# A two-block transformer kernel: output norms, gate and first key and query tiles taken token tile by token tile

## The reference, cut to what matters

```python
h = h + rms_norm(y, norm_post[i])        # y = o @ w_out, 1024x1024
e = p[i] @ ple_w[i]                      # 256 features -> 1024
g = sigmoid(h @ ple_gate[i])             # 1024x1024
h = h + rms_norm(g * e, ple_norm[i])
```

## Time and profile before

| | us |
|---|---|
| median of 3 runs (1077.23 to 1079.66) | 1077.61 |
| the profiled execution | 1082.48 |
| its span on the core | 1080.7 |

### The profile page before, as it was taken

The page is one execution under the profiler, slowest core; times in us unless marked ns, Lnnn a source line. Parts: engine busy times, 40 slices in busy tenths (PEclk is TensorE's granted clock), DMA queues, the critical chain, the costliest instruction groups (busy, mean ns, idle before and its releaser), DMA issues.

```text
span 1080.7 us, 20360 instructions
## 1 busy us (share of the span) xinstructions
PE 1036.0 (96%) x8578; PEld 870.3 (81%) x8578; DVE 485.1 (45%) x668; ACT 558.8 (52%) x888; POOL 747.4 (69%) x470
## 2 busy tenths in 40 slices
PE   7999999999999999999999999999999999999796
PEld 6887898999989969999998456699977787777665
DVE  3125176431146876421145848544467344223433
ACT  6548365444446956444443434222335368578744
POOL 5986468998865678998883175440327777998863
PEclk9999899999999999999999999999999999999999
DMA  9771345556545644555556335300004463554241
GB/s 360 269 252 60 126 160 178 183 192 191 182 164 169 200 170 162 187 194 181 190 189 225 132 123 177 129 4 4 5 23 156 154 211 134 199 176 133 82 162 43
DMA packets 46218, 168.36 MB, mean 156 GB/s; under 512 B 5648, under 2 KB 5904, under 8 KB 45872
## 3 DMA queue, kind: packets, MB, share of 16 engines
q1 hardware_dynamic: 43616, 158.02, 43.2%
q0 software_dynamic: 2512, 9.05, 2.5%
HBM read 166.00 MB, written 1.05 MB: 155 GB/s over the span
## 4 chain that ended last, share of the span: by engine, by line
PE 82%; ACT 7%; DVE 6%; issue 2%; DMA 1%; SPq 0%; POOL 0%; DVEq 0%; ACTq 0%
PE psum L443 29%; PE psum L480 18%; PE psum L702 16%; PE psum L2255 5%; PE psum L455 3%; PE psum L2403 1%; PE psum L252 1%; ACT high_r L962 1%; DMA h<-x 1%; PE psum L1989 1%; PE psum L2143 1%; DVE arena L1516 1%; PE psum L227 1%; PE psum L2321 1%; ACT arena L1009 0%
## 5 line engine op out<-in xcount | busy, mean ns | idle before, releaser
L792 POOL TENSOR_TENSOR ring_r<-ring,high_r 128x512 fp32r<-128x512 f32 (+1 forms) x374 | 647.0, 1762 | 157.9 <-ACT high_r L962 144.1
L962 ACT CAST high_r<-ring 128x1024 fp32r<-128x1024 f32 x250 | 257.8, 1049 | 187.0 <-DMA ring<-w 182.9
L480 PE MATMUL psum<-x_high,high_r 128*128 128x256 f32 x640 | 183.0, 286 | 2.8 <-DVE x_low L316 2.8
L480 PE MATMUL psum<-x_low,high_r 128*128 128x256 f32 x640 | 181.7, 284 | 0.0
L480 PE MATMUL psum<-x_high,ring_r 128*128 128x256 f32 x640 | 181.7, 284 | 0.0
L674 DVE TENSOR_TENSOR arena<-arena 128x512 f32<-128x512 f32 x32 | 47.7, 1490 | 193.9 <-ACT arena L650 193.8
L480 PEld LDWEIGHTS psum<-x_high,high_r 128*128 128x128 f32 x640 | 123.5, 193 | 4.1 <-issue 3.5
L480 PEld LDWEIGHTS psum<-x_low,high_r 128*128 128x128 f32 x640 | 123.6, 193 | 0.5
L480 PEld LDWEIGHTS psum<-x_high,ring_r 128*128 128x128 f32 x640 | 123.5, 193 | 0.0
L443 PE MATMUL psum<-high_r,x_high 128*128 128x512 f32 x256 | 102.3, 399 | 7.2 <-POOL ring_r L787 2.4
L702 PE MATMUL psum<-high_r,zz_high 128*128 128x512 f32 x256 | 99.8, 390 | 1.3 <-DVE zz_low L681 1.3
(11 more groups left out here) (360 smaller groups left out, 1826.2 us busy)
## 6 DMA issues: line engine op xcount, KB each, us to landing
ring<-w SPq DMA_DIRECT2D x288, 512.0 KB, 3.3
row<-rows POOLq DMA_DIRECT2D x14, 512.0 KB, 6.3
arena<-relt SPq DMA_DIRECT2D x2, 1536.0 KB, 14.0
h<-x SPq DMA_DIRECT2D x1, 1024.0 KB, 11.3
arena<-lora POOLq DMA_DIRECT2D x2, 512.0 KB, 7.1
out<-h SPq DMA_DIRECT2D x2, 512.0 KB, 2.6
arena<-xT SPq DMA_DIRECT2D x1, 768.0 KB, 6.6
con<-consts SPq DMA_DIRECT2D x1, 529.0 KB, 7.0
```

What stands on the lines that cost most here:

```text
L480: ins = nc.tensor.matmul(out, a, b, start=(k == 0 and q == 0), stop=(k == KT - 1 and q == 2))
L792: ins = nc.gpsimd.tensor_tensor(low(m)[:, part], raw(m)[:, part], read(high(m))[:, part], ALU.subtract)
L962: nc.scalar.copy(high(m), raw(m)).then_inc(high_made, 1)
```

## The change

`out_by_token` walks the second output tile for all of t = 0 and then all of t = 1; sum, root, reciprocal and addition to `h` follow for each token tile by itself. The embedding product is split in two column halves, of which the first needs only the first output tile read; the three matmuls without use go. The transposes of `h` are made for one token tile at a time in banks of four blocks (`pe_token_transposes`), t = 0 between the halves, t = 1 inside the first gate tile, which is now walked by token tile too. The first key and query tiles are walked t = 0 of the keys, transposes of t = 1, t = 0 of the queries, t = 1 of the keys, t = 1 of the queries; `kv_high`, `q_high`, `kv_low` and `q_low` make the parts by token tile with 128x128 instructions. A piece of a tile that is walked by token tile is given back (`piece_used`) in the pass of t = 1. The matmuls without use are now 22 ahead of the transposes of t = 0 and 12 behind them. `posted` moves in the arena, and in `embed_dve` the gain of the second column half comes after the variance.

```diff
+            def out_by_token(first, e_n):
+                for t in range(NT):
+                    for i in range(4):
+                        piece_ready(pe, 4 * (first + 1) + i)
+                        ins = pe_piece_of_tile(pe, first + 1, i, 2, xT2, t)
+                        if t == 1:
+                            ins.then_inc(piece_used, 1)
+                    if t == 0:
+                        ins.then_inc(out_pass, 1)
...
             def embed_pe(tile, e_n, T):
-                hold_clock(4, 3)
-                pe.wait_ge(part_sq, 8 * e_n + 4)
-                pe.wait_ge(part_gain, 4 * e_n + 4)
...
+                embedding_half(tile, e_n, 0)
+                pe_token_transposes(pe, T, h, 0, posted_rows)
+                embedding_half(tile, e_n, 1).then_inc(piece_used, 4)
+                for t in range(NT):
+                    for i in range(4):
+                        if t == 0 and i == 3:
+                            pe_token_transposes(pe, T, h, 1, posted_rows)
...
-            hold_clock(0, 8)
-            pe_transposes_of_tile(pe, T_H7, h, 0, token_ready(0))
-            hold_clock(0, 14)
-            pe_transposes_of_tile(pe, T_H7, h, 1, token_ready(1))
+            hold_clock(0, 22)
+            pe.wait_ge(gate_act, 1)
+            pe_token_transposes(pe, T_H7, h, 0, embedded_rows)
+            hold_clock(0, 12)
...
+            for t in range(NT):
+                for c in range(2):
+                    for i in range(4):
+                        piece_ready(pe, 4 * (W_KVQG + c) + i)
...
+                        ins = pe_piece_of_tile(pe, W_KVQG + c, i, KVQG_BANK[c], KVQG_X[c], t)
+                        if t == 1:
+                            ins.then_inc(piece_used, 1)
+                    if (t, c) == (0, 0):
+                        pe.wait_ge(gate_act, 3)
+                        pe_token_transposes(pe, T_H7, h, 1, embedded_rows)
```

On ScalarE, `out_norm` has the casts of the first two gate pieces behind the root of each token tile, and the stretch behind the embedding reads:

```diff
+                    if e_n == 0 and t == 1:
+                        kv_high(0)
...
             out_norm(6, W_OUT_A, 0)
             embed(7, W_PLE0, 0, T_H6)
             split_until(4 * W_KVQG + 5)
+            q_high(0)
             split_until(4 * W_KVQG + 8)
+            kv_high(1)
+            q_high(1)
```

More of the change, by code:

```diff
@@ L1844, in out_gain @@
-            def out_gain(i, first, e_n, name):
-                g_ = row_of(name)
[L1847 to L1852, removed]
-                        nc.vector.tensor_tensor(posted[:, t, hl], psum[:, 2 * c + t, :], g_[:, hl], ALU.mult).then_inc(part_gain, 1)
-                dve.wait_ge(part_gain, 4 * e_n + 4)
-                add_normed(i, 2 * e_n)
@@ new lines, in kv_low @@
+            def kv_low(t):
+                tt = slice(t * P, (t + 1) * P)
+                for b in range(4):
+                    dve.wait_ge(xb_high_made, 4 * t + 2 * (b // 2) + 2)
+                    for k in (2 * b, 2 * b + 1):
+                        ins = nc.vector.scalar_tensor_tensor(out=XBL[:, k, tt], in0=token_filling(4 * T_H7 + 2 * t + b // 2)[:, k % 4, :],
+                                                             scalar=c8("kv_norm")[:, k:k + 1], in1=read(XBH[:, k, tt]),
+                                                             op0=ALU.mult, op1=ALU.subtract)
+                    ins.then_inc(xb_low_made, 1)
@@ new lines, in q_low @@
+            def q_low(t):
+                tt = slice(t * P, (t + 1) * P)
+                for q in range(2):
+                    g = 4 * T_H7 + 2 * t + q
+                    dve.wait_ge(tp_act, ACT_BANKS[g + 1])
+                    for k in range(4 * q, 4 * q + 4):
+                        ins = nc.vector.scalar_tensor_tensor(out=XL[:, k, tt], in0=token_filling(g)[:, k % 4, :],
+                                                             scalar=c8("norm_pre1")[:, k:k + 1], in1=read(XH[:, k, tt]),
+                                                             op0=ALU.mult, op1=ALU.subtract)
+                    ins.then_inc(tp_dve, 1)
@@ L2388, in _, with embedding_half @@
             gate_piece(1, 3)
+            def out_by_token(first, e_n):
[5 more added lines that the diff above has]
+                            ins.then_inc(piece_used, 1)
+                    if t == 0:
+                        ins.then_inc(out_pass, 1)
+            def embedding_half(tile, e_n, c):
+                pe.wait_ge(part_sq, 8 * e_n + 2 * c + 2)
+                pe.wait_ge(part_gain, 4 * e_n + 2 * c + 2)
+                for k in range(2):
+                    for t in range(NT):
+                        ins = nc.tensor.matmul(psum[:, 2 * c + t, :], pT_sb[:, k, t * P:(t + 1) * P],
+                                               raw(4 * tile + k)[:, c * HALF:(c + 1) * HALF], start=(k == 0), stop=(k == 1))
+                return ins
@@ L2411, in embed_pe @@
+                embedding_half(tile, e_n, 1).then_inc(piece_used, 4)
+                for t in range(NT):
+                    for i in range(4):
+                        if t == 0 and i == 3:
+                            pe_token_transposes(pe, T, h, 1, posted_rows)
+                        piece_ready(pe, 4 * (tile + 1) + i)
+                        bank_out(pe, 4 * T + 2 * t + i // 2)
                         ins = pe_piece_of_tile(pe, tile + 1, i, 4, xT2, t)
-                    ins.then_inc(piece_used, 1)
+                        if t == 1:
+                            ins.then_inc(piece_used, 1)
```

201 lines of the change are left out of this document (112 added, 89 removed).

## The result

| us | before | changed |
|---|---|---|
| median | 1077.88 (1077.23 to 1079.66, 4 runs) | 1088.46 (1085.46 to 1093.11, 4 runs) |
| profiled execution | 1082.48 | 1087.55 |
| its span | 1080.7 | 1085.5 |
| mean granted clock | 0.994 | 0.992 |

A forecast was written before the change was run, and what follows sets the result against it. TensorE, in matmuls for 96% of the span, was taken as the bound, so time is won only where it stands still or works for nothing. 7.8 lost less 2.1 won gives +5.7 us, 1077.61 to 1083.3, range 1078.0 to 1086.0.

The forecast's parts named there:

- Output tile and embedding, first boundary: Second output tile to gate's end, first boundary: tile ends 0.4 late, gate ends at 885.4, 1.7 us won.
- From the gate to the keys: Gate's end to first key matmul: matmuls without use decide, keys start at 894.2 against 896.62, 2.4 us won.
- The supply of pieces: First key and query passes: POOL supplies 243 to 247 late, TensorE stands about one us before each of four or five passes.
- The release of the ring, and POOL behind it: From the keys' second pass: late release of 240 and 241 delays evacuation, rotation and piece 252; 7.8 us lost.
- Load 3.3: Ring release step: load assumed to take 3.3 us before cast 1.05 and evacuation 0.7, giving 919.1.
- Second boundary: Output tile to gate at the second boundary: no 0.4 wait for POOL, 2.1 us won.
- A (faster): Rival: POOL has the low part of 247 by 904.6, both boundary wins stand, 1074.0 us; chance 0.08.
- B (no change): Rival: supply in time, only late release counts, or slack behind 939 returns most of the 7.8; 1078.0 us; chance 0.14.
- C (the clock falls): Rival: clock falls in the starved stretch from 899 to 910, delaying release of 241 by 1.7; 1085.0 us; chance 0.14.
- The sum: Whole kernel: +7.8 - 2.1 = +5.7 us, put on the median 1077.61, giving 1083.3.

The follow-up runs named there:

- e9: Changed kernel with 15 instead of 22 matmuls without use ahead of the transposes of t = 0; 1085.14 us, ratio 1.0042.
- e8: e7 with 15 instead of 22 matmuls without use ahead of the transposes of t = 0; 1076.14 us, ratio 0.9961.
- e5: Changed kernel with ScalarE casting pieces 243 to 245 ahead of the keys' high parts of t = 0; 1082.16 us, ratio 1.0009.
- e3: Changed kernel with ScalarE evacuating the first key tile ahead of the casts of pieces 248 and 249; 1082.62 us, ratio 1.0017.
- after_again: The changed kernel, unedited, run once more with a profile of its own; 1086.86 us, ratio 1.0054.
- e4: Changed kernel with 20 matmuls without use added in TensorE's pause before piece 248; 1088.19 us, ratio 1.0067.
- e2: Changed kernel with both key passes by token tile first, then the queries piece by piece; 1082.93 us, ratio 1.0011.
- e7: Changed kernel with the edits of e2, e5 and e3 together; 1075.73 us, ratio 0.9974.
- e6: Changed kernel with the edits of e5 and e3 together; 1078.17 us, ratio 0.9989.

## Why the prediction was right and wrong

The direction, the place and the mechanism were right, the size too small: a load was put at 3.3 and took 4.6 to 5.6, and the clock that falls in the longer pause behind it was left out. All times below count from the end of the second output tile, since the absolute ones carry what earlier stages did (851.49 after, 854.38 before).

**Output tile and embedding, first boundary.** Forecast 1.7 won by the gate's end with a tile that ends 0.4 late. Measured: TensorE waits 0.25 for POOL at 844.39, before the fourth piece (forecast 0.4), and from tile's end to gate's end 2.2 are won (forecast 10.8 - 7.9 - 0.9 = 2.0, and with the wait 1.7). The high parts of `h` for t = 1, put at nothing, cost nothing: TensorE has no wait in the gate.

**From the gate to the keys.** Forecast 39.4 to the first key matmul, measured 890.18 - 851.49 = 38.7. That the matmuls without use decide is right: `h` was ready at 885.25 (VectorE's 883.14 and 2.11) and the transposes began at 886.71. e9 took 1.6 of it away. The margin to `h` is 1.5, and in e8, where the sum into `h` takes 3.17, it is used up.

**The supply of pieces.** Right in its pattern: four waits for POOL of 0.8 to 1.2 (above). The eight key parts took 2.17 (forecast 2.3), POOL's run of ten began at 892.67 - 851.49 = 41.2 (42.0) and ended at 54.3 (55.1), and 241 was given back at 58.7 (59.2). e5, which supplies the pieces, removed 5.2 of the stretch and with it every one of these waits.

**The release of the ring, and POOL behind it.** This is the step that was mis-sized. Its form was right: two casts wait for a load, the evacuation stands behind them, POOL's rotation behind that, and POOL's list decides the rest. e3 shows the blocked evacuation by moving it. But "Load 3.3" was 5.59 for piece 249. The same load took 4.77 in after_again and 4.58 in e4; in e5 and e9 the chain passes through the load of a later piece, 5.66 and 5.24. The load of 248, issued 1.36 ahead of it, took 3.2 (908.86 to the cast at 912.09). With 241 back 0.5 early, the rotation started at 66.05 instead of 64.3 (at 65.2 in after_again and 65.1 in e4). The transfers of the changed kernel between 903 and 927:

```profile
issues: line engine op xcount, KB each, median us to landing
ring<-w SPq DMA_DIRECT2D x8, 512.0 KB, 5.2
```

A pass in which a piece is used for the last time gives a piece back every 1.36 us, and 0.524 MB in 1.36 us would be 385 GB/s. That is close to all that was ever moved: 326 from 910 to 920 at a DMA share of 0.95, and at most 412 in any 5 us between 900 and 940 of these profiles (e4, 917 to 922, share 1.01). Before, a piece came back every 2.7 us, and the median of ten loads between 895 and 925 was 3.3. I took the duration of a load from a stretch in which they meet less. That their meeting made this one longer is argued from these rows; no run varies it by itself, and why the same load took 1.0 more in one profile than in another is open.

The second miss of this step: "TensorE is at 252 at 937.1, ahead of POOL by 1.7. So POOL decides". The pause before 248 was 5.38 instead of 3, the granted clock was 0.57 from 925 to 930, mostly the lower of its two levels (1.2 GHz), and the 24 matmuls of 248 and 249 took 8.33 instead of 5.5. That used up the 1.7 and 1.1 more; e4 gives the 1.1 back. From the output tile to 252 the forecast was 84.2 and the profile has 938.37 - 851.49 = 86.9: the excess of 2.7 is 1.7 of the load and 1.0 of the clock. In after_again the excess is 1.9, since its load was shorter.

**Second boundary.** Forecast 2.1, measured 2.0 to the gate's end and 2.1 to the end of the span.

**Rivals.** A (faster) and B (no change) fall by the stretch of 93.2. B's slack behind 939 isn't there: all kernels with the second boundary's edit take 140.6 to 141.2 from the first scores on. C (the clock falls) was right that it falls and wrong in the place. It called the starved stretch busy by half; TensorE was busy for 6.47 of the 9.00 us from 898.3 to 907.3. In bursts of 1.4 with pauses of 0.8 to 1.2 the clock stayed at 1.00 from 900 to 910, in all five profiles that have them (those of after, after_again, e3, e4, e9); it fell after the single pause, of 5.38 (4.58, 4.22 and 5.38 in after_again, e9 and e5). But a short pause is not safe as such: in e2 it fell behind pauses of 1.23 and 1.94 with a burst between them, and in the kernel before behind pauses of 0.99 and 1.28 around 324 us, while it stayed at 1.00 behind 1.73 in e3 and 1.53 in e7. What sets these apart the runs don't show. By the Trainium skill (TensorE: Matmul & The Clock Gate, HAM oscillation) it is long waits for a load between bursts that bring the clock down, so that the next burst starts slow. The trace agrees for the pause of 5.38; the case described there has no pauses as short as those of the starved stretch, so it doesn't by itself ask for the 1085.0 that the forecast drew from it.

**The sum.** Forecast +5.7. The profiles give +9.7 - 2.1 = 7.6, the first four runs 8.2 (1.0076), the later twelve 5.8 (1.0054). The mechanism as sized by the profiles would be 2 us above the forecast; how much of the rest of the difference between the two samples is the varying clock of whole runs isn't settled, and the interval of the first goes from 4.3 to 12.2. As a difference the range was +0.4 to +8.4: the 10.6 between the first medians lies above it, the 8.2 and the 5.8 of the ratios within. That the later ratio meets the forecast's 5.7 is luck, since its own profile has 9.0 lost (92.4 - 83.5) and 1.7 won, 7.3. The range reached only 1 us past C, and had no term for a load slower than the row it was taken from, though the text itself said that a load slower by 1.5 would show elsewhere.

## What to carry to other kernels

When a walk order is changed, work out for the ring not only when a piece is wanted but when it is given back, and how close together: places that come back in a bunch are loaded in a bunch, and here a load then took longer than the median of a calm stretch. Look for anything that stands on a queue behind a prefetch that can now block; here one evacuation behind two casts cost 4.5 us, and moving it was one line. A new wait of several microseconds on TensorE is to be priced with the slow restart behind it, and the slack that hides it is to be counted after that. Work that is moved ahead to feed one engine can slow another: the early casts gave 5.2 us, and made the sum into `h` 1.1 longer.

## What the runs showed of the hardware that was not expected

- Of eight loads of 512 KB issued 1.36 us apart, the first took 3.2 us, the second 4.6 to 5.6 and later ones up to 5.7 (326 GB/s over 10 us); where they came every 2.7 us the median was 3.3.
- TensorE in bursts of 1.4 us with pauses of 0.8 to 1.2 us (busy 6.47 of 9.00 us) kept a granted clock of 1.00 in five profiles; a pause of 5.4 us was followed by 0.57 for 5 us. In e2 pauses of 1.23 and 1.94 us were followed by 0.66 and 0.50.
- VectorE's sum of two 128x1 values (L1943) took 1.19 us at 879.95, with POOL in its low parts, and 0.15 at 890.67, with POOL idle:

```profile
879.95 1.19 DVE L1943 TENSOR_TENSOR small<-small 128x1 f32<-128x1 f32 x1 [0.86 <-ACT arena L1284]
...
890.67 0.15 DVE L1943 TENSOR_TENSOR small<-small 128x1 f32<-128x1 f32 x1
```

  That agrees with the Trainium skill (SBUF — State Buffer, SBUF: two separate sides), by which an operation of VectorE with both inputs in SBUF waits while GpSimd holds the ports that they share. POOL's run ended between the two. The sum into `h`, which also reads two tensors in SBUF, took 3.17 for its two instructions in e5, e6 and e8, where POOL's low parts ran beside it but for 0.44 (e7: 3.16), and 2.11 in the changed kernel, where they ended during it (877.31 + 6.72 = 884.03).
- Fifteen matmuls without use in place of 22 ahead of the transposes left the granted clock at 1.00 from 870 to 900 in the profiles of e8 and e9.
